# Gate tiles of a mixed attention and recurrence block: all sixteen placed between the steps of the two mixers

## The chip, the core and the metric

The kernel runs on one core of a Trainium2 chip. It uses the five engines of the core: PE (TensorE, matmuls), DVE (VectorE), ACT (ScalarE), POOL (GpSimd) and SP (SyncE, which here only issues DMAs). Each engine works through its own instructions in the order in which they are written and waits on semaphores. The metric is the device time of one execution in microseconds; lower is better.

## The reference, cut to what matters

Two transformer blocks are computed for 512 tokens of width 1024. The part that the change touches is the input projection of the second block's mixer, and the two mixers that use it:

```python
proj = u @ w_in                 # 1024 -> 5256 columns
(q_a, c_kv, q_idx, k_idx, w_idx, q_h, f_h, i_h, g_h, gate_a, gate_b) = split_cols(proj)
# sparse attention: a score per key picks the 128 best keys of each query
dots = einsum('bqhd,bsd->bqhs', qi, k_idx)
score = einsum('bqh,bqhs->bqs', wi, relu(dots)); score = where(causal, score, -inf)
_, idx = lax.top_k(score, 128)
# softmax over the chosen keys, 8 heads, latent values
# recurrence (hgrn2): 4 heads, chunkwise, decay from a running sum of log f
merged = sigmoid(gate_a + b) * (y_a @ w_br_a) + sigmoid(gate_b + b) * (y_b @ w_br_b)
h = h + rms_norm(merged @ w_out, g)
```

The two gates (2048 of the columns) are used only in the last but one line. Nothing in either mixer needs them.

## The kernel before

Activations lie transposed, features on partitions and the 512 tokens along the free axis. A projection is cut into output tiles of 128 columns. A tile takes 8 pieces, one for each 128 inputs, and a piece is three matmuls of 128x512 (high weights by high activations, high by low, low by high, lines 721 to 723 or, in `fill`, 743 to 745), since each operand is split into two parts. The weights of a tile (a unit) are loaded by SP into one of four slots, ACT makes the high part (`w_hi`, L1142) as soon as the tile three before it is finished, and POOL or DVE makes the low part (`w_lo`, L633 on POOL, L1711 and L2278 on DVE).

The second block's input projection has 43 tiles, `TILES2`: numbers 0 to 26 feed the mixers, 27 to 42 are the sixteen gate tiles. The first `LEAD2` tiles are computed one after the other; this is called the front here. Behind a tile, the list `AFTER2` places small work: transposes, latent queries and the index scores. An index score is a matmul of PE (L996), a relu of ACT (L1451) and a multiply-add of DVE (L2161) that adds it to the score. There are 24 of them in 12 pairs: eight for each of the query blocks 3, 2 and 1. Between them DVE picks the best keys of the block just finished: `top8` (L2143 finds eight maxima, L2144 takes them out) 16 times for each block. Before, all 16 rounds for block 1 stand behind the whole front, and `selected(1)` (L2148) ends them.

In the front DVE also moves each mixer tile out of its bank (L2128). ACT works in order too: behind a tile it makes `w_hi`, then waits for DVE's move, applies silu or sigmoid, issues the store, and only then the relus of that tile's index scores.

The sparse attention (35 steps `a`, 8 heads by 4 query blocks) has, in each step on PE, the logits of step a (L1005), the transposes of step a-2 (L1012), the pieces `FILL2[a]` of gate tiles, and the values of step a-3 (L1026); every eighth step a projection (L1036). The logits go to DVE (L2197 adds bias and mask, which POOL prepares at L686), ACT (exponential, L1466), and DVE (L2214, attn). Step 35 of the table has 14 pieces: they stand between the sparse attention and the recurrence.

The recurrence has 36 steps, 4 heads by 9 levels l. On PE each step has the pair matmuls (L1078) and then its pieces; the first step of a head has other pair matmuls ahead (L1065); at level 2 the output of the head before follows the pieces (`hgrn_out`, L1055). POOL makes differences (L663, L665), ACT decays (L1517, L1521, L1522), DVE the factors (L2259, L2260) and keeps the pairs (`keep_pairs`, L2268). At level 4 ACT keeps the output of the head before (L1501), and behind level 5 it takes the logarithm for the next head (`log_forget`, L1507, between two table loads); with it DVE makes the running sums (L2246, three scans) behind level 6.

A finished gate tile costs ACT `keep_gate`: `w_hi` of a later unit, a copy out of the bank (L1410) and the issue of a store. In the recurrence ACT does it two steps after the tile was finished, behind the decay of that step; in the sparse attention one step after.

Of the kernel before, what the change touches and what calls it, by code (L numbers as in the profile page):

```python
# [51 lines left out]
TOPK = 128  # L52
# [17 lines left out]
for _name, _n in (("norm_mix_g", 8), ("norm_ffn_g", 8), ("norm_final_g", 8), ("pool_scale", 4),  # L70
# [10 lines left out]
TILES2 = (["ckv", "kidx", "widx"] + [f"qi{t}" for t in range(4)] + [f"qa{t}" for t in range(4)]  # L81
          + [f"i{t}" for t in range(4)] + [f"qh{t}" for t in range(4)] + [f"gh{t}" for t in range(4)]
          + [f"fh{t}" for t in range(4)] + [f"gate{t}" for t in range(16)])
# [1 line left out]

TILES1 = [(kind, h) for h in range(HEADS) for kind in "qkv"] + [("p", g) for g in range(len(WINDOWS))]
LEAD1 = 3
LEAD2 = TILES2.index("gate0") + 4
STAGES = (("proj1", 16, DC), ("wo", DC, DC), ("up1", 2 * FC, DC), ("down1", 2 * DC, DOWN_CHUNKS),
          ("up2", 2 * FC, DC), ("down2", 2 * DC, DOWN_CHUNKS), ("proj2", len(TILES2), DC),  # L90
          ("branch", 2 * DC, 4), ("out", DC, DC),
# [16 lines left out]
def spread(first_tile, end_tile, rates):  # L108

    steps, at, end = [], first_tile * DC, end_tile * DC  # L110
    for rate in rates:
        pieces, left = [], min(rate, end - at)
        while left:
            n = min(left, DC - at % DC)
            pieces.append((at // DC, at % DC, at % DC + n))
            at, left = at + n, left - n
        steps.append(pieces)
    assert at == end, (at, end)
    return steps


def closed(pieces):
# [6 lines left out]
DSA_STEPS = DSA_HEADS * QB  # L129
HGRN_STEPS = HEADS * len(LEVELS)  # L130
GAP2 = DSA_STEPS + 3
_rates = [1 + (a % 5 == 4) for a in range(GAP2)] + [14]
_left = (len(TILES2) - LEAD2) * DC - sum(_rates)
FILL2 = spread(LEAD2, len(TILES2), _rates + [
    _left * (e + 1) // HGRN_STEPS - _left * e // HGRN_STEPS for e in range(HGRN_STEPS)])
# [78 lines left out]
for _t in range(4):  # L214
    AFTER2[8 + _t] += [("qlat", 2 * _t), ("qlat", 2 * _t + 1)]
    AFTER2[12 + _t].append(("vturn", _t))
_room = TILES2.index("gate0") - 1 - 7
for _s in range(len(IDX_STEPS)):
    AFTER2[7 + _s // 2 * _room // (len(IDX_STEPS) // 2 - 1)].append(("idx", _s))
for _n in AFTER2:  # L220
# [91 lines left out]
def two_blocks(nc, ins, spill, bias_rows, out):  # L312

    with ExitStack() as ctx:
# [162 lines left out]
        def tile_read(stage, i):  # L477
            return tile_sem(stage, i), TILE[stage, i][1] + 1
# [148 lines left out]
        def _(pool):  # L627
# [7 lines left out]
            def split_units(name, start, end):  # L635

                first, size = UNIT[name][0], UNIT[name][2] * P
                loops = max(0, end - start) // SLOTS
                if loops > 1:
                    with pool.Fori(0, loops) as it:  # L640
                        for j in range(SLOTS):
                            split_unit(first + start + j, size, it, SLOTS)
                    start += SLOTS * loops
                for i in range(start, end):
                    split_unit(first + i, size)
# [24 lines left out]
            pool.wait_ge(unit_split, UNIT["proj2"][0] + SLOTS)  # L670
            split_units("proj2", SLOTS, LEAD2 + 3)

# [26 lines left out]
        def _(pe):  # L699
            mm = nc.tensor.matmul  # L700

            def wait(pair):
                pe.wait_ge(pair[0], pair[1])
# [246 lines left out]
            for i in range(AUX_BANKS):  # L950
                wait(tile_read("up2", i))
            for n in range(LEAD2):
                if n == 0:
# [176 lines left out]
        def _(act):  # L1130
# [282 lines left out]

            for n, name in enumerate(TILES2[:LEAD2]):
                kind, t = name.rstrip("0123456789"), int(name[len(name.rstrip("0123456789")):] or 0)
# [222 lines left out]
        def _(dve):  # L1638
# [3 lines left out]
            def step(ins_, it=0, per_loop=0):  # L1642

                steps[0] += 1
                ins_.then_inc(dve_step, 1)
                dve.wait_ge(dve_step, steps[0] + (it * per_loop if per_loop else 0))
# [188 lines left out]
            for name, factor in (("attn_norm_g", 1.0 - LAM_INIT), ("ffn1_post_g", 0.5), ("ffn2_post_g", 0.5)):  # L1835
                first, n = PARAMS[name]
# [294 lines left out]
            def norm_keys(name):  # L2131

                n, src, dst, g = {"ckv": (0, ckv_raw, ckv, "kv_norm_g"),
                                  "kidx": (1, kidx_raw, kidx, "kidx_norm_g")}[name]
                rsqrt(name)
                wait(tile_read("proj2", n))
                v.scalar_tensor_tensor(dst[:, :], src[:, :], prm(g), rstd[:, :], ALU.mult, ALU.mult).then_inc(
                    norm_ready, 1)
                dve.wait_ge(norm_ready, n + 1)

            def top8(i):

                step(v.max(best[:, :], score[i][:, :]))  # L2143
                step(v.match_replace(score[i][:, :], best[:, :], score[i][:, :], TAKEN))  # L2144
# [24 lines left out]
                    if h == DSA_HEADS - 1:  # L2169
                        selected(i + 1)  # L2170
            dve.wait_ge(const2_loaded, 16 * 3)
            for n in range(TILES2.index("gate0")):
                take_tile2(n)
                for ev, m in AFTER2[n]:
                    if ev == "spread":
                        norm_keys(m)
                    elif ev == "wturn":
                        dve.wait_ge(aux_ready, AUX["wturn", 0] + 1)
                        v.tensor_scalar(widx[:, :, :],
                                        aux_bank("wturn", 0)[:, 0:32].rearrange("p (j h) -> p j h", j=QB),  # L2180
                                        IDX_W_SCALE, None, ALU.mult).then_inc(aux_sem("wturn", 0), 1)
                        wait(aux_read("wturn", 0))
                    elif ev == "idx":
                        index_step(m)
            for _r in range(TOPK // 8):
                top8(1)
            selected(1)

            for a in range(DSA_STEPS + 4):
# [156 lines left out]
            for c in range(2):  # L2346
                dve.wait_ge(p_loaded, 32)
                n = SPLIT["p"] + c
# [128 lines left out]
```

## Time and profile before

| | us |
|---|---|
| median of 3 runs | 2026.54 (2024.76 to 2027.18) |
| the profiled execution | 2031.31 |
| its span | 2029.4 |

| engine | busy us | share of the span |
|---|---|---|
| PE | 1861.8 | 92% |
| DVE | 1167.6 | 58% |
| ACT | 648.5 | 32% |
| POOL | 201.2 | 10% |

PE's clock (PEclk) is shown as a share of full speed: 1.0 is 2.4 GHz, 0.5 is 1.2 GHz, and a figure between is a mean over a stretch with both. A wait is idle time of an engine, put down to the instruction that released it. In these profiles the durations of back-to-back matmuls overlap (a matmul of 0.39 us starts every 0.23 us at full clock), so the time of a piece is read from start to start.

### The profile page before, as it was taken

Reading aid. Unit: us, or ns where it says so; the run is one execution under the profiler, and the core shown is the slowest. Engines: PE = TensorE matmul, PEld = TensorE weight load, DVE = VectorE, ACT = ScalarE, POOL = GpSimd, SP = SyncE. Lnnn points to the kernel's source line nnn. Section 1 sums busy time; section 2 is a strip of 40 time slices with the busy share of each in tenths; the row PEclk is TensorE's granted clock in tenths of the full one; section 3 lists DMA queues with packets and bytes.
Section 4 is the critical chain, followed back from the end, with each engine's and each line's share of the span. In section 5 each row is a group of like instructions: output and inputs, shape, how many; then the busy total and the mean of one; then the engine's idle time right before and its main releaser. Section 6 shows DMA issues by size and latency. Waiting matters only on the chain.

```text
span 2029.4 us, 23515 instructions
## 1 busy us (share of the span) xinstructions
PE 1861.8 (92%) x8254; PEld 1489.2 (73%) x8254; DVE 1167.6 (58%) x1772; ACT 648.5 (32%) x960; POOL 201.2 (10%) x150
## 2 busy tenths in 40 slices
PE   5887989999999999999899998877789999999996
PEld 4665777777888888888677776666567788888874
DVE  6447658888534755532443776576683755452266
ACT  4333412222223222222333334444353322222242
POOL 3121000000000000000033344243000000000000
PEclk9888999999999999999899999977899999999997
DMA  3431222223222222323222331310152222232221
GB/s 136 79 67 42 73 80 89 92 92 101 100 98 83 93 93 97 103 100 100 78 83 73 114 129 59 114 68 32 47 161 83 73 96 101 93 119 100 92 71 54
DMA packets 55340, 180.61 MB, mean 89 GB/s; under 512 B 6216, under 2 KB 6984, under 8 KB 55272
## 3 DMA queue, kind: packets, MB, share of 16 engines
q1 hardware_dynamic: 43200, 157.07, 23.2%
q10 hardware_dynamic: 12072, 22.67, 4.0%
q8 instruction: 39, 0.64, 0.1%
q14 instruction: 29, 0.24, 0.0%
HBM read 167.65 MB, written 12.06 MB: 89 GB/s over the span
## 4 chain that ended last, share of the span: by engine, by line
PE 68%; DVE 19%; issue 6%; ACT 3%; DMA 2%; POOL 1%; DVEq 1%; ACTq 0%; SPq 0%; POOLq 0%
PE bank L721 16%; PE bank L722 16%; PE bank L723 16%; PE bank L743 2%; PE bank L744 2%; PE bank L809 2%; PE bank L745 2%; PE bank L810 2%; PE bank L811 2%; DMA raw<-in_w_proj 1%; DVE sq L1990 1%; PE bank L1078 1%; PE bank L789 1%; DVE w_lo L1711 1%; DVE chunk L1809 1%
## 5 line engine op out<-in xcount | busy, mean ns | idle before, releaser
L1142 ACT ACTIVATE w_hi<-raw 128x1024 fp32r<-128x1024 f32 (+2 forms) x281 | 304.4, 1087 | 742.7 <-PE bank L723 677.8
L721 PE MATMUL bank<-a_hi,w_hi 128*128 128x512 f32 x1272 | 504.1, 396 | 17.9 <-DVE w_lo L1711 7.7
L723 PE MATMUL bank<-a_hi,w_lo 128*128 128x512 f32 x1272 | 496.8, 391 | 0.0
L722 PE MATMUL bank<-a_lo,w_hi 128*128 128x512 f32 x1272 | 496.5, 390 | 0.0
L1711 DVE TENSOR_TENSOR w_lo<-raw,w_hi 128x1024 fp32r<-128x1024 f32 (+2 forms) x219 | 280.4, 1281 | 246.7 <-ACT w_hi L1142 234.2
L721 PEld LDWEIGHTS bank<-a_hi,w_hi 128*128 128x128 f32 x1272 | 239.9, 189 | 87.9 <-issue 19.7
L723 PEld LDWEIGHTS bank<-a_hi,w_lo 128*128 128x128 f32 x1272 | 239.7, 188 | 50.7
L722 PEld LDWEIGHTS bank<-a_lo,w_hi 128*128 128x128 f32 x1272 | 240.1, 189 | 49.4 <-issue 1.0
L633 POOL TENSOR_TENSOR w_lo<-raw,w_hi 128x1024 fp32r<-128x1024 f32 x54 | 130.5, 2419 | 1103.9 <-ACT w_hi L1142 1103.9
L721 PE MATMUL bank<-h_hi,w_hi 128*128 128x512 f32 x568 | 221.1, 389 | 0.2 <-DVE w_lo L1711 0.2
L723 PE MATMUL bank<-h_hi,w_lo 128*128 128x512 f32 x568 | 221.0, 389 | 0.0
L722 PE MATMUL bank<-h_lo,w_hi 128*128 128x512 f32 x568 | 221.0, 389 | 0.0
L721 PEld LDWEIGHTS bank<-h_hi,w_hi 128*128 128x128 f32 x568 | 106.6, 188 | 22.8 <-issue 0.6
L723 PEld LDWEIGHTS bank<-h_hi,w_lo 128*128 128x128 f32 x568 | 106.6, 188 | 22.1
L722 PEld LDWEIGHTS bank<-h_lo,w_hi 128*128 128x128 f32 x568 | 106.6, 188 | 21.9
L743 PE MATMUL bank<-a_hi,w_hi 128*128 128x512 f32 x240 | 111.7, 466 | 2.0 <-DVE w_lo L2278 1.2
L744 PE MATMUL bank<-a_lo,w_hi 128*128 128x512 f32 x240 | 99.0, 413 | 0.0
L745 PE MATMUL bank<-a_hi,w_lo 128*128 128x512 f32 x240 | 98.9, 412 | 0.0
L809 PE MATMUL bank<-a_hi,w_hi 128*128 128x512 f32 x144 | 61.6, 428 | 38.8 <-POOL w_lo L633 19.4
L2059 DVE TENSOR_TENSOR val<-bank,rstd 128x512 f32<-128x512 f32 x44 | 30.4, 691 | 115.4 <-PE bank L723 115.4
L1078 PE MATMUL bank<-qk 128*128 128x128 f32 (+1 forms) x256 | 46.2, 330 | 27.6 <-DVE qk L2260 27.5
L809 PEld LDWEIGHTS bank<-a_hi,w_hi 128*128 128x128 f32 x144 | 29.4, 204 | 51.8 <-issue 21.4
(291 smaller groups left out, 2255.3 us busy)
## 6 DMA issues: line engine op xcount, KB each, us to landing
raw<-in_w_up SPq DMA_DIRECT2D x132, 512.0 KB, 3.4
raw<-in_w_down SPq DMA_DIRECT2D x48, 704.0 KB, 4.0
raw<-in_w_proj SPq DMA_DIRECT2D x59, 512.0 KB, 3.5
raw<-in_w_wo SPq DMA_DIRECT2D x8, 512.0 KB, 3.4
raw<-in_w_branch SPq DMA_DIRECT2D x16, 256.0 KB, 2.7
gates_in<-spill ACTq DMA_DIRECT2D x16, 256.0 KB, 3.0
raw<-in_w_out SPq DMA_DIRECT2D x8, 512.0 KB, 4.3
raw<-in_w_ple SPq DMA_DIRECT2D x8, 512.0 KB, 3.5
```

What stands on the lines that cost most here:

```text
L633: pool.tensor_tensor(lo, src, hi.bitcast(F32), ALU.subtract).then_inc(unit_split, 1)
L721: mm(dst[:, :], wh, hi[:, k, :], start=(first and c == 0), stop=False)
L722: mm(dst[:, :], wh, lo[:, k, :], start=False, stop=False)
L723: step = mm(dst[:, :], wl, hi[:, k, :], start=False, stop=(last and c == n - 1))
L743: mm(dst[:, :], wh, a_hi[:, c, :], start=(c == 0), stop=False)
L744: mm(dst[:, :], wh, a_lo[:, c, :], start=False, stop=False)
L745: step = mm(dst[:, :], wl, a_hi[:, c, :], start=False, stop=(c == DC - 1))
L809: mm(dst[:, :], wh, hi[:, k, :], start=(k == 0), stop=False)
L810: mm(dst[:, :], wh, lo[:, k, :], start=False, stop=False)
L1078: step = mm(dst[:, col:col + n], qk[:, e % 2, j * P:(j + 1) * P], qk[:, e % 2, q0:q0 + n], start=True, stop=True)
L1142: fn(w_hi[:, slot, 0:size], raw[:, slot, 0:size], ACT.Copy).then_inc(unit_high, 1)
L1711: v.tensor_tensor(w_lo[:, slot, 0:size], raw[:, slot, 0:size], w_hi[:, slot, 0:size].bitcast(F32), ALU.subtract).then_inc(unit_split, 1)
```

## The change

`LEAD2` becomes 27 instead of 31: the front ends with the last mixer tile, and all sixteen gate tiles are computed piece by piece between the steps. The table of pieces changes with it. The sparse attention gets 1 piece in even steps and 2 in odd ones, 52 in all (before 42: 2 in each fifth step, else 1). The 14 pieces of step 35 stay. The recurrence gets 62 pieces (before 40), which is 1 or 2 in a step: by level 1 2 2 1 2 2 2 1 2 in heads 0 and 2, and 2 1 2 2 2 1 2 2 2 in heads 1 and 3 (before 1 1 1 1 1 1 1 1 2 in each).

The 12 pairs of index scores stand behind tiles 7 8 10 11 13 14 16 17 19 20 22 24 (before 7 8 10 12 13 15 17 19 20 22 24 26), and the 16 rounds of `top8` for block 1 stand behind tiles 25 and 26, eight behind each. The tiles, their banks and SP's queue are the same.

```diff
-LEAD2 = TILES2.index("gate0") + 4
+LEAD2 = TILES2.index("gate0")
...
-_rates = [1 + (a % 5 == 4) for a in range(GAP2)] + [14]
+_rates = [1 + a % 2 for a in range(GAP2)] + [14]
...
-_room = TILES2.index("gate0") - 1 - 7
+_room = LEAD2 - 3 - 7
...
-            for n in range(TILES2.index("gate0")):
+            for n in range(LEAD2):
                 take_tile2(n)
...
-            for _r in range(TOPK // 8):
-                top8(1)
+                for _r in range(TOPK // 16 if n >= LEAD2 - 2 else 0):
+                    top8(1)
             selected(1)
```

DVE at the end of the front. Before, block 2 is finished and the rounds of block 1 (score_113) follow at once, both evictions being long done:

```order
L2148 TENSOR_SCALAR score_114<-score_114 128x384
L2143 MAX best<-score_113 128x8
L2144 MATCH_REPLACE score_113<-best,score_113 128x256
L2143 MAX best<-score_113 128x8
L2144 MATCH_REPLACE score_113<-best,score_113 128x256
```

Now the eviction of tile 25 stands in between:

```order
L2148 TENSOR_SCALAR score_114<-score_114 128x384
L2128 TENSOR_TENSOR gate<-bank,rstd_mix 128x512
L2143 MAX best<-score_113 128x8
L2144 MATCH_REPLACE score_113<-best,score_113 128x256
```

The eviction of tile 26 stands eight rounds later. The index scores ahead of this place have moved two tiles forward.

PE in head 1 of the recurrence, levels 1 and 2 (qk are the factors of a level, bank1 holds the gate tile). Before, one piece of three matmuls stands behind each pair matmul, and hgrn_out (pair_d by v2) follows:

```order
L1078 MATMUL bank5<-qk_135 128x128 x4
L743 MATMUL bank1<-a_hi_53,w_hi_51 128x512
L744 MATMUL bank1<-a_lo_54,w_hi_51 128x512
L745 MATMUL bank1<-a_hi_53,w_lo_50 128x512
L1078 MATMUL bank6<-qk_135 128x128 x4
L743 MATMUL bank1<-a_hi_53,w_hi_51 128x512
L744 MATMUL bank1<-a_lo_54,w_hi_51 128x512
L745 MATMUL bank1<-a_hi_53,w_lo_50 128x512
L1055 MATMUL bank2<-pair_d_136,v2_101 128x128 x2
L1055 MATMUL bank2<-pair_1_137,v2_101 128x128
```

Now level 2 has two pieces ahead of hgrn_out, as level 0 has:

```order
L1078 MATMUL bank5<-qk_135 128x128 x4
L743 MATMUL bank1<-a_hi_53,w_hi_51 128x512
L744 MATMUL bank1<-a_lo_54,w_hi_51 128x512
L745 MATMUL bank1<-a_hi_53,w_lo_50 128x512
L1078 MATMUL bank6<-qk_135 128x128 x4
L743 MATMUL bank1<-a_hi_53,w_hi_51 128x512
L744 MATMUL bank1<-a_lo_54,w_hi_51 128x512
L745 MATMUL bank1<-a_hi_53,w_lo_50 128x512
L743 MATMUL bank1<-a_hi_53,w_hi_51 128x512
L744 MATMUL bank1<-a_lo_54,w_hi_51 128x512
L745 MATMUL bank1<-a_hi_53,w_lo_50 128x512
L1055 MATMUL bank2<-pair_d_136,v2_101 128x128 x2
```

What moved: six more pieces stand in this head, at levels 0, 2, 3, 4, 6 and 7.

ACT in head 1, levels 4 to 6. Before, the kept output (oh, sq) and the decay of level 5 are followed by the logarithm (silu<-hf, between its table loads) and the decays of level 6:

```order
L1501 ACTIVATE oh<-bank 128x512
L1186 ACTIVATE sq<-oh 128x512
L1517 ACTIVATE decay<-diff 128x512
L1507 ACT_TABLE_LOAD
L1507 ACTIVATE silu<-hf 128x512
L1521 ACT_TABLE_LOAD
L1521 ACTIVATE decay<-diff 128x4x64
```

Now the work for a finished gate tile stands in between:

```order
L1501 ACTIVATE oh<-bank 128x512
L1186 ACTIVATE sq<-oh 128x512
L1517 ACTIVATE decay<-diff 128x512
L1142 ACTIVATE w_hi<-raw 128x1024
L1410 ACTIVATE gate<-bank 128x512
L1412 DMA spill<-gate 128x512
L1507 ACT_TABLE_LOAD
L1507 ACTIVATE silu<-hf 128x512
L1521 ACT_TABLE_LOAD
L1521 ACTIVATE decay<-diff 128x4x64
```

It stands at the same place in head 0. In head 2, where such work stood there before, it now stands behind the decays of level 6.

## Rows read from the trace of the kernel before

**Rows 1.** The page, part 4: the chain that ended last, shares by engine.

```profile
PE 68%; DVE 19%; issue 6%; ACT 3%; DMA 2%; POOL 1%; DVEq 1%; ACTq 0%; SPq 0%; POOLq 0%
```

**Rows 2.** Busy time by stretch of the span; columns as its header row says.

```profile
core 0: us, PE busy (x) PEld busy (x) DVE busy (x) ACT busy (x) POOL busy (x), PEclk, DMA share, GB/s
1106.00:1190.00 84.00, 79.82 (x357) 61.69 (x355) 60.79 (x113) 28.52 (x42) 31.15 (x13) 0.99 0.36 119
1190.00:1218.80 28.80, 26.81 (x108) 21.55 (x108) 23.94 (x67) 10.33 (x14) 12.45 (x7) 0.91 0.36 128
1218.80:1303.50 84.70, 72.54 (x398) 55.09 (x399) 60.11 (x163) 42.34 (x110) 36.70 (x35) 0.98 0.18 57
1323.00:1446.00 123.00, 93.99 (x504) 80.78 (x504) 82.60 (x128) 49.62 (x86) 42.74 (x60) 0.82 0.12 41
1422.60:1443.80 21.20, 20.47 (x142) 18.32 (x142) 13.92 (x25) 8.84 (x18) 4.72 (x7) 1.00 0.13 37
```

**Rows 3.** Waits of DVE, 1106 to 1218.5 us: total us, times, longest us.

```profile
DVE score L2161 <- ACT relu L1451: 19.1, 6, 3.7
DVE score L2158 <- ACT relu L1451: 2.8, 2, 1.5
```

**Rows 4.** Timeline, DVE, ACT and PE, end of the front: start us, us, what, [idle before].

```profile
1189.88 0.69 DVE L2128 TENSOR_TENSOR gate<-bank,rstd_mix 128x512 f32<-128x512 f32 x1
...
1190.60 0.63 ACT L1427 ACTIVATE gate<-gate 128x512 f32<-128x512 f32 x1 [6.45 <-DVE gate L2128]
...
1190.62 0.79 PE L721 MATMUL bank<-a_hi,w_hi 128*128 128x512 f32 x1 [4.80 <-DVE gate L2128]
...
1192.07 0.63 PE L721 MATMUL bank<-a_hi,w_hi 128*128 128x512 f32 x1
...
1193.35 0.63 PE L721 MATMUL bank<-a_hi,w_hi 128*128 128x512 f32 x1
...
1194.14 1.33 DVE L2161 SCALAR_TENSOR_TENSOR score<-relu,widx,score 128x256 f32<-128x256 f32 x1 [2.97 <-ACT relu L1451]
...
1197.57 0.39 PE L721 MATMUL bank<-a_hi,w_hi 128*128 128x512 f32 x1
...
1198.25 0.39 PE L721 MATMUL bank<-a_hi,w_hi 128*128 128x512 f32 x1
...
1217.99 0.45 DVE L2148 TENSOR_SCALAR score<-score 128x256 f32<-128x256 f32 x1
...
1221.83 0.30 PE L1012 MATMUL bank<-ident,attn 128*128 128x128 f32 x1 [4.39 <-DVE attn L2214]
```

**Rows 5.** Waits in the sparse attention, 1218.8 to 1303.5 us: PE's, then DVE's.

```profile
PE bank L1012 <- DVE attn L2214: 13.5, 10, 4.4
...
DVE logit L2197 <- PE bank L1005: 12.4, 11, 1.8
DVE logit L2197 <- PE bank L1012: 6.3, 7, 1.5
```

**Rows 6.** Waits in the recurrence, 1323 to 1446 us: PE's, DVE's, ACT's.

```profile
PE bank L1078 <- DVE qk L2260: 27.5, 15, 5.8
...
DVE pair_d L2268 <- PE bank L1065: 15.5, 3, 5.7
...
ACT oh L1501 <- PE bank L1055: 11.0, 3, 5.0
```

**Rows 7.** Timeline, recurrence, ACT, PE and DVE: start us, us, what, [idle before].

```profile
1374.12 1.04 ACT L1142 ACTIVATE w_hi<-raw 128x1024 fp32r<-128x1024 f32 x1
...
1375.06 1.21 PE L1078 MATMUL bank<-qk 128*128 128x128 f32 x8 [2.14 <-DVE qk L2260]
...
1399.98 0.61 ACT L1142 ACTIVATE w_hi<-raw 128x512 fp32r<-128x512 f32 x1
...
1405.51 0.88 DVE L2259 TENSOR_TENSOR qk<-hk,decay 128x256 f32<-128x256 f32 x1 [3.49 <-issue]
...
1406.87 2.05 PE L1078 MATMUL bank<-qk 128*128 128x128 f32 x8 [3.52 <-DVE qk L2260]
```

## The prediction

> **What bounds the kernel now.** I read the chain of waits first, by engine: PE holds 68% of it and DVE 19% [rows 1]. So PE's work, and what PE waits for, set the end. Then I read the stretches that the change touches [rows 2]. In the front, 1106 to 1190, PE is busy 79.82 of 84.00 us. From 1190 to 1218.8 it is busy 26.81 of 28.80, but with work that nobody waits for, the four gate tiles, while DVE finishes the choice of keys (23.94 busy). The sparse attention (1218.8 to 1303.5) has PE busy 72.54 of 84.70 us, at a clock of 0.98, and the recurrence (1323 to 1446) 93.99 of 123.00 at a mean clock of 0.82. PE's idle time lies there, 12 and 29 us, and the question is how much of the four tiles fits into it.
>
> The reader should see two prices in the timeline at the end of the front [rows 4]. A piece, from the start of L721 to the next, takes 0.68 us at full clock (1197.57 to 1198.25), and 1.28 us at half clock (1192.07 to 1193.35), where PE starts again after a wait of 4.80 us. And the front does not end with PE: DVE's last instruction for the choice (L2148) is at 1217.99, and PE waits 4.39 us until 1221.83 for the first attn.
>
> **The front.** Four tiles leave it, 32 pieces, 21.8 us of PE at full clock. None of this is saved as such, since the sparse attention starts when DVE is done. What counts is how much sooner DVE is done. Its work is the same: the same evictions, 24 multiply-adds and 48 rounds. Only its idle time can shrink. From 1106 to 1218.8 that is 28 us (112.8 less 60.79 and 23.94 busy) [rows 2], of which 21.9 us are waits for relus, 19.1 and 2.8 [rows 3]; the rest is waits for PE and short gaps. The cause is visible [rows 4]: DVE evicts fh2 at 1189.88 and fh3 behind it, ACT only then starts (0.63 us at 1190.60), stores, does the next, and the relu comes so late that DVE resumes at 1194.14 after 2.97 idle us. This order on ACT is unchanged. I went through the new order by hand. Of the pairs from tile 13 on, the one at tile 14 follows a tile without silu and finds its relus ready; those at 17 and 20 stand behind a single eviction, where the relu is some 1.8 us late instead of 3.0 to 3.7 (estimate: one silu, one issue and half a pair of relus less); 16, 19, 22 and 24 wait 3.5 to 4.3. Their sum is about 20 us, 2 less than before, and about 2 us of waits for PE's tiles go as well, since DVE is then behind PE. I take **-4 us**. The ends are 0 (the waits only move) and -22 (all waits for relus go). The eight rounds behind tile 25 do not stall anything: by then PE's tile 26 is finished or in work, and its bank is another.
>
> PE's restart at the head of the sparse attention stays. Now it comes after 4.39 us of idle time, later after some 25 us. A wait of 4.80 us is enough to bring PE back at half clock, as the pieces at 1192.07 and 1193.35 show [rows 4], so I count nothing more for the longer one; 2 us is the upper end (three pieces at 1.28 instead of 0.68).
>
> Here a rule speaks against the change. The Trainium skill, "TensorE: Matmul & The Clock Gate", section "HAM oscillation — how this bites in real kernels", says that an array with long idle gaps falls back to half rate and pays a restart after each. By the rule alone the new gap would be charged those 2 us; by the rows the old gap had already paid them. The trace agrees with the rule as far as the restart at 1190.62 goes [rows 4].
>
> **The sparse attention.** Ten pieces more, 6.8 us of PE. PE waits 13.5 us in 10 places there, 4.4 of it at the start [rows 5], so about 9 us could take them; but DVE waits for PE's logits as well, 12.4 and 6.3 us, so PE and DVE hold each other. It depends on the step. The waits of PE come mostly at steps with a%4 = 0. A second piece in a%4 = 3 stands just ahead of one and is mostly hidden: 7 more pieces, of which I count 1.3 us. In a%4 = 1 it delays the logits of the next block, which DVE waits for: 7 more pieces, 4.8 us. Four even steps lose a piece, -2.5. The sum is **+3.5 us**; ends 0 and 6.8. POOL has two more splits here and ACT one or two more tiles to keep. POOL is busy 36.70 of 84.70 us, ACT 42.34, so I cost them at nothing; if a split of POOL got in front of a mask that DVE wants, it would cost up to 2.4 us each.
>
> **Between.** The 14 pieces, the loads of the recurrence and its first scans are unchanged: nothing.
>
> **The recurrence.** 22 pieces more, 15 us at full clock, and three more tiles for ACT to keep. PE waits here 27.5 us in 15 places for the factors [rows 6], which looks like room for everything. But the waits lie in the wrong levels. DVE waits 15.5 us, 3 times, for the pair matmuls that open a head (L1065), and ACT 11.0 us, 3 times, for hgrn_out (L1055). So in each head PE's pieces at levels 7 and 8 and at levels 0 to 2 are on the path, and those at 3 to 6 are beside it: there the path goes through ACT, from the kept output over decay, two table loads and the logarithm to the level 6 decays, and then through DVE's scans. By head:
> - Head 0 has no hgrn_out; its added pieces at 1, 2, 4, 5 and 6 meet small waits, and the first piece need no longer wait for its low part: +0.5.
> - Head 1: levels 0 (partly at half clock, 1.0), 2 (0.7) and 7 (half, 1.3): +3.0.
> - Head 2: levels 1 and 2: +1.4.
> - Head 3: there is no next head to prepare, and PE is busy 20.47 of 21.20 us at full clock [rows 2]; six pieces are 4.1 us, less 0.7 of idle time: +3.4.
>
> That makes 8.3 us. Then ACT. Keeping a tile costs w_hi 1.04 us [rows 7], a copy of some 0.6 and the issue with its gap, 2.1 us in all. In heads 0 and 1 this now stands just ahead of the logarithm. The trace has this case in head 2: ACT does w_hi at 1399.98 (a small unit, 0.61 us) between decay and logarithm, DVE's factors come 3.49 us late at 1405.51, and PE waits 3.52 us at 1406.87, where in head 1, without such work, it waits 2.14 (1375.06) [rows 7]. So twice +2.1, and -1.5 in head 2, where the work moves behind the level 6 decays and under the scans: +2.7. Two more splits on DVE (1.2 us each) fall where it waits anyway. The recurrence gives **+11 us**; its ends are -5 (a higher clock, below) and +18 (every piece at full price and the 2.7).
>
> **The sum.** -4 + 3.5 + 11 = +10.5 us. The profiled execution was 2031.31 us, with 1.9 outside its span; it would become 2041.8. It is 4.8 us above the median of the runs, 2026.54, and I expect the same difference of the runs: **2037.0 us**. What a measurement can tell from no change is 0.2%, 4.1 us.
>
> **Rivals.**
> - *DVE stops waiting in the front (faster).* If closer pairs let each relu be ready when DVE gets to it, all 22 us of waits go, DVE is done near 1196, and the change is -22 + 3.5 + 11 = -7.5: 2019.0 us. For it: DVE is busy 60.79 of 84.00 us only [rows 2], and the pairs stand closer. Against it: ACT's relu stands behind DVE's eviction of the same tile, whatever the distance. It decides from a gain of 14.5 us in the front upwards (3.5 + 11): below that the mixers take it back.
> - *The clock stays up in the recurrence (no change).* The mean clock of 0.82 over 123.00 us means about 44 us at half rate. If the denser pieces shorten the waits ahead of level 6 (2.14 and 3.52 us [rows 7]) so that the clock no longer falls after them, and half of those 44 us run at full rate, PE is 11 us sooner. The sum is -4 + 3.5 + 11 - 11 = -0.5: 2026.0. For it: in head 3, without long waits, the clock is 1.00. Against it: the scans keep their wait, and ACT's added work lengthens those of heads 0 and 1.
> - *Nothing is hidden (slower still).* 6.8 in the attention, 15 and 2.7 in the recurrence, and a second of POOL's splits in the way, 2: +22.5 with the front's -4, 2049 us. For it: PE and DVE wait for each other in both mixers. Against it: 27.5 us of waits, some of which must take in the added pieces.
> - *The front gains 10, the recurrence loses 7:* +0.5, 2027. Each term is at its good side, but no mechanism of its own stands behind it.
>
> **How the numbers follow.** My own forecast 0.60, with a range of 2030 to 2043; the faster front 0.10; the clock 0.12; nothing hidden 0.10; the mixed case 0.08. Ends that hold 8 in 10: 2024 to 2047. Faster by over 0.2%: the first rival and a third of the clock's, 0.14. Within 0.2%: 0.08 of the clock's and 0.07 of the mixed case, 0.15. Slower: mine, nothing hidden and 0.01 of the mixed case, 0.71.
>
> **What would show it.** In the changed kernel: DVE's L2148 for block 1 at about 1213 to 1215, with waits for relus of 18 to 20 us; PE idle from about 1187 until then; the sparse attention 3 to 4 us longer than 84.7, with PE's waits for attn down to 8 or so; the recurrence 10 us or more longer than 123, with PE's waits in it smaller, DVE's waits for L1065 longer, and the level 6 factors of heads 0 and 1 later by 2 us. If the mean clock there rises above 0.9, the second rival is right. If L2148 comes before 1206, the first is. A front that ends later than now would prove my pass over it wrong.

## The result and the profile after

The changed kernel takes 2036.83 us (median of 5 runs, 2035.63 to 2038.77), the kernel before 2026.54 (5 runs): ratio 1.0057, 95% interval 1.0043 to 1.0071, so 10.3 us slower. Forecast were 2037.0. The sum hides a loss that I had at nothing, a gain that I had too small and a loss that I had too large.

To see where the time went I cut the span at the same instructions in both traces. The profiled executions took 2038.77 us (after) and 2031.31 (before), 1.9 and 4.8 above their medians: they are 7.5 us apart where the medians are 10.3, so the table holds some 3 us less than there is to explain.

| stretch, from the first instruction of one line to that of the next | before | after | difference | forecast |
|---|---|---|---|---|
| ahead of the front | 1041.4 | 1039.6 | -1.8 | 0 |
| front: first scaling of the latent keys on DVE to the first logit, L2197 | 177.4 | 170.4 | -7.0 | -4 |
| sparse attention: to the last value projection, L1036 | 91.0 | 95.6 | +4.6 | +3.5 |
| gap: to the first L1065 | 10.0 | 20.3 | +10.3 | 0 |
| first scans and factors: to the first L1078 | 7.0 | 4.0 | -3.0 | 0 |
| recurrence: to the last hgrn_out, L1055 | 116.8 | 119.3 | +2.5 | +11 |
| behind it, to the end of the span | 585.8 | 587.6 | +1.8 | 0 |

The stretches of the changed kernel, with the columns of the header row:

```profile
core 0: us, PE busy (x) PEld busy (x) DVE busy (x) ACT busy (x) POOL busy (x), PEclk, DMA share, GB/s
1106.00:1210.00 104.00, 85.78 (x365) 65.75 (x363) 83.66 (x179) 31.73 (x47) 33.98 (x15) 0.92 0.29 101
1210.00:1218.80 8.80, 5.67 (x18) 3.89 (x18) 6.17 (x18) 2.79 (x9) 4.10 (x5) 0.60 0.00 0
1210.00:1305.70 95.70, 84.51 (x461) 64.97 (x461) 63.09 (x163) 46.28 (x116) 41.77 (x37) 0.96 0.20 67
1305.70:1329.90 24.20, 13.56 (x54) 10.46 (x51) 7.83 (x12) 7.43 (x9) 4.77 (x8) 0.78 0.55 206
1329.90:1425.20 95.30, 73.60 (x410) 62.58 (x410) 67.52 (x101) 40.27 (x68) 32.69 (x45) 0.91 0.16 54
1425.20:1449.40 24.20, 24.16 (x160) 21.91 (x160) 14.65 (x26) 8.80 (x18) 4.89 (x7) 1.00 0.12 41
```

The fourth row is the surprise: 24.20 us with PE busy 13.56. The last row is head 3, with PE full, as before in 21.20 us [rows 2].

**Front.** DVE's waits in the changed kernel, 1106 to 1210 (total us, times, longest), and the timeline at its end (start us, us, what, idle before):

```profile
DVE score L2161 <- ACT relu L1451: 11.9, 5, 3.0
DVE score L2158 <- ACT relu L1451: 4.2, 2, 3.0
```

```profile
1192.71 0.69 DVE L2128 TENSOR_TENSOR gate<-bank,rstd_mix 128x512 f32<-128x512 f32 x1
...
1209.64 0.29 DVE L2148 TENSOR_SCALAR score<-score 128x256 f32<-128x256 f32 x1
1209.96 0.29 DVE L2197 TENSOR_TENSOR logit<-bank,sum_sq 128x128 f32<-128x128 f32 x1
...
1213.13 0.44 PE L1012 MATMUL bank<-ident,attn 128*128 128x128 f32 x1 [16.24 <-DVE attn L2214]
...
1213.23 0.77 PE L743 MATMUL bank<-a_hi,w_hi 128*128 128x512 f32 x1
1213.80 0.63 PE L744 MATMUL bank<-a_lo,w_hi 128*128 128x512 f32 x1
```

The waits for relus are 16.1 us against 21.9 [rows 3], 5.8 less where I had 2, and L2148 stands at 1209.64 where I had 1213 to 1215 (before: 1217.99 [rows 4]). PE waits 16.24 us, not some 25, since it has work until 1196.9 where I had 1187, and starts at half clock (0.63 us a matmul; mean 0.60 in the second row above). The Trainium skill, "TensorE: Matmul & The Clock Gate", section "HAM oscillation — how this bites in real kernels", says that a long gap is paid for with a restart; this trace agrees (0.63 us a matmul behind 16.24 us without work), and e4_rec72 below has the price.

**Between.** The end of the gap in the changed kernel, ACT, PE and DVE:

```profile
1313.14 0.91 DVE L2228 MEMSET pair_d<- 128x1024 f32 x1 [5.40 <-DMA resets<-in_c_resets]
...
1315.57 3.45 DVE L2246 TENSOR_TENSOR_SCAN run<-resets,silu 128x512 f32<-128x512 f32 x3 [0.30 <-ACT silu L1507]
...
1321.99 1.04 ACT L1142 ACTIVATE w_hi<-raw 128x1024 fp32r<-128x1024 f32 x1
1322.94 0.58 ACT L1410 ACTIVATE gate<-bank 128x512 f32<-128x512 f32 x1
...
1323.57 0.80 PE L743 MATMUL bank<-a_hi,w_hi 128*128 128x512 f32 x1 [8.94 <-ACT gate L1410]
...
1326.30 1.91 PE L1065 MATMUL bank<-hq,hk 128*128 128x128 f32 x8
1328.24 0.72 DVE L2268 COPY_PREDICATED pair_d<-masks,bank 128x512 f32<-128x512 int32 x1 [9.22 <-PE bank L1065]
```

Read it from below. DVE waits 9.22 us for the first pair matmuls, these stand behind two pieces, and the first of these waits 8.94 us until ACT has copied a gate tile out of its bank. The gate tiles share two banks in turn. Before, 42 + 14 = 56 pieces are seven whole tiles, and the 14 of step 35 finish the seventh. Now 52 + 14 = 66: the 14 finish tiles 33 and 34 and put two pieces into tile 35, whose bank is that of tile 33. ACT empties tile 33 only in the recurrence, behind the decay of its step 1, and that decay needs DVE's scans. The 14 pieces were unchanged; where they stand against the tile's end was not.

**Recurrence.** Starts of level 0 (L1078), head by head, one execution each:

| | head 0 | head 1 | head 2 | head 3 | PEclk, heads 0 to 2 |
|---|---|---|---|---|---|
| before, 40 pieces | 32.2 | 30.4 | 33.2 | 21.3 | 0.78 |
| after, 62 | 32.8 | 32.6 | 29.9 | 24.2 | 0.91 |

Head 3 is longer by 2.9 (forecast 3.4). Heads 0 to 2 have 16 pieces more and are together half a microsecond shorter (forecast 7.6 longer).

### The profile page after: what moved, and what is told of

It reads as the page before. It is cut to its first block, busy times and chain, and to the rows that moved or that the text cites. A ratio compares the mean times of both kernels' runs of the same rounds, so it can differ in the third digit from the quotient of the medians.

```text
span 2036.8 us, 23512 instructions
## 1 busy us (share of the span) xinstructions
PE 1855.9 (91%) x8254; PEld 1484.8 (73%) x8254; DVE 1171.5 (58%) x1774; ACT 648.6 (32%) x960; POOL 196.3 (10%) x148
## 4 chain that ended last, share of the span: by engine, by line
PE 68%; DVE 20%; issue 6%; DMA 3%; ACT 3%; DVEq 1%; POOL 1%; ACTq 0%; SPq 0%; POOLq 0%
PE bank L721 16%; PE bank L723 16%; PE bank L722 16%; PE bank L743 2%; PE bank L745 2%; PE bank L744 2%; PE bank L809 2%; PE bank L810 2%; PE bank L811 2%; DMA raw<-in_w_proj 2%; DVE score L2144 1%; DVE best L2143 1%; DVE sq L1990 1%; PE bank L1078 1%; PE bank L789 1%
## 5 line engine op out<-in xcount | busy, mean ns | idle before, releaser
L721 PEld LDWEIGHTS bank<-a_hi,w_hi 128*128 128x128 f32 x1240 | 234.2, 189 | 81.0 <-issue 20.4
L723 PEld LDWEIGHTS bank<-a_hi,w_lo 128*128 128x128 f32 x1240 | 234.3, 189 | 50.0
L722 PEld LDWEIGHTS bank<-a_lo,w_hi 128*128 128x128 f32 x1240 | 234.4, 189 | 48.3 <-issue 1.0
L633 POOL TENSOR_TENSOR w_lo<-raw,w_hi 128x1024 fp32r<-128x1024 f32 x52 | 125.8, 2420 | 1102.4 <-ACT w_hi L1142 1102.4
L723 PEld LDWEIGHTS bank<-h_hi,w_lo 128*128 128x128 f32 x568 | 106.6, 188 | 21.9
L2059 DVE TENSOR_TENSOR val<-bank,rstd 128x512 f32<-128x512 f32 x44 | 30.4, 690 | 115.6 <-PE bank L723 115.6
L743 PEld LDWEIGHTS bank<-a_hi,w_hi 128*128 128x128 f32 x272 | 54.1, 199 | 24.8 <-ACT gate L1410 9.4
L809 PEld LDWEIGHTS bank<-a_hi,w_hi 128*128 128x128 f32 x144 | 29.6, 206 | 48.3 <-issue 20.6
```

What stands on the lines that cost most here:

```text
L633: pool.tensor_tensor(lo, src, hi.bitcast(F32), ALU.subtract).then_inc(unit_split, 1)
L721: mm(dst[:, :], wh, hi[:, k, :], start=(first and c == 0), stop=False)
L722: mm(dst[:, :], wh, lo[:, k, :], start=False, stop=False)
L723: step = mm(dst[:, :], wl, hi[:, k, :], start=False, stop=(last and c == n - 1))
L743: mm(dst[:, :], wh, a_hi[:, c, :], start=(c == 0), stop=False)
L809: mm(dst[:, :], wh, hi[:, k, :], start=(k == 0), stop=False)
```

## The experiments

Three theories went in: A, the bank wait makes the loss of the gap; B, the pieces in the mixers lie on the path as forecast; C, the loss comes from PE standing idle at the end of the front, where it had four gate tiles to do before. Each result has the kernel before as run on the same chip beside it: 2027.07 (e1 to e4), 2026.62 (e5 to e8), 2026.03 (e9, e10, e12), 2025.38 (e13).

### e1_gap12 and e2_keep33: the bank

```diff
-_rates = [1 + a % 2 for a in range(GAP2)] + [14]
+_rates = [1 + a % 2 for a in range(GAP2)] + [12]
```

> The changed kernel with 12 instead of 14 pieces between the mixers; the recurrence gets 64 instead of 62. Theory A (bank): the last 2 of the 14 pieces open tile 35, which needs the bank of tile 33, and ACT empties that bank only in the recurrence. The 12 pieces end with tile 34, so the wait of 8.94 us goes and the first pair matmuls no longer stand behind it. The recurrence starts 9 to 10 us sooner: 2026 to 2029 us. Theory B (pieces in the recurrence are on its path, as predicted): two more pieces there cost 1 to 2 us: 2038 us. Theory C (the loss is the front's missing cover, the idle PE): no change, 2037 us.

```diff
+            early = closed(FILL2[GAP2])[:1]
+            for t in early:
+                keep_gate(t)
             log_forget(0)
...
-                            keep_gate(t)
+                            if t not in early:
+                                keep_gate(t)
```

> The changed kernel with its 14 pieces, but ACT copies tile 33 out of its bank before the first logarithm of the recurrence, not two steps into it. PE's order is the same. Theory A (bank): PE's wait of 8.94 us goes to under 1 us: 2026 to 2029 us. Theories B and C: no change, 2035 to 2039 us; ACT's two us fall into its wait for the loads.

Measured: e1 2027.41 us, ratio to before 1.0000 [0.9991, 1.0008]; e2 2030.79, 1.0019 [1.0010, 1.0028]. The first pair matmuls and the first factors of e1, with PE released by DVE's keys and DVE waiting for nothing from PE:

```profile
1316.94 1.13 PE L1065 MATMUL bank<-hq,hk 128*128 128x128 f32 x8 [0.74 <-DVE hk L2239]
1317.10 3.46 DVE L2246 TENSOR_TENSOR_SCAN run<-resets,silu 128x512 f32<-128x512 f32 x3 [0.30 <-ACT silu L1507]
1320.47 0.70 DVE L2268 COPY_PREDICATED pair_d<-masks,bank 128x512 f32<-128x512 int32 x1
```

Gap and first factors are 16.9 us in e1 and 16.7 in e2, as before (17.0), against 24.3 in the changed kernel. e2 changes nothing but when the bank is emptied: the wait costs 6.0 us by the medians. e1 came within theory A's range of 2026 to 2029, e2 1.8 us above it and 4.2 below the range of B and C. So A has the cause, and its size was too large: the loss of the gap is 7.3 us in the traces and 6.0 by the medians, not 9 to 10. The rest of e1's gain is the next experiment's term.

### e5_defer: ACT's tile ahead of the logarithm

e2_keep33, and the tiles due at level 5 are kept behind the decays of level 6 (the diff is against e2_keep33):

```diff
-                        for t in closed(FILL2[GAP2 + e - 1]):
+                        late = closed(FILL2[GAP2 + e - 2]) if l == 6 else []
+                        for t in late + (closed(FILL2[GAP2 + e - 1]) if l != 5 else []):
```

> The changed kernel with tile 33 kept by ACT before the first logarithm (as in e2_keep33, 2030.79 us), and with ACT's keep_gate of level 5 moved behind the decays of level 6. In heads 0 and 1 it no longer stands between decay and logarithm. Theory ACT (my prediction: such a tile costs 2.1 us of the path, twice): 4.2 us less than e2_keep33, 2026.6. Theory beside (PE's own work sets those heads, so that factors that come 2 us sooner are taken up 2 us later by PE): within 1 us of e2_keep33, 2030 to 2031.5. Trace: by theory ACT, PE's longest wait for factors in heads 0 and 1 shrinks from some 3.5 to some 1.5 us.

Measured: 2027.60 us, 3.2 below e2 (expected by theory ACT 4.2 below, by its rival at most 1). Head 1, first e2, then e5: level 6's factors and pair matmuls.

```profile
1365.85 1.06 ACT L1142 ACTIVATE w_hi<-raw 128x1024 fp32r<-128x1024 f32 x1 [0.50 <-PE bank L745]
...
1371.83 0.88 DVE L2263 TENSOR_TENSOR qk<-hk,decay 128x256 f32<-128x256 f32 x1 [4.51 <-ACT decay L1525]
...
1373.20 1.13 PE L1078 MATMUL bank<-qk 128*128 128x128 f32 x4 [3.51 <-DVE qk L2264]
```

```profile
1367.15 1.04 ACT L1142 ACTIVATE w_hi<-raw 128x1024 fp32r<-128x1024 f32 x1
...
1367.33 0.88 DVE L2264 TENSOR_TENSOR qk<-hk,decay 128x256 f32<-128x256 f32 x1 [2.10 <-ACT decay L1525]
...
1368.69 1.13 PE L1078 MATMUL bank<-qk 128*128 128x128 f32 x8 [1.09 <-DVE qk L2265]
```

PE's wait falls from 3.51 to 1.09. Heads 0 and 1 are 2.5 and 2.4 us shorter, head 2 1.4 longer though nothing was moved in it, 3.5 in all, close to the medians (3.2). e1 needs neither mend, since its tiles end elsewhere, and agrees with e5: 2027.4 and 2027.6. So after (2036.8) is e1 plus the bank (6.0) plus this term (3.2).

### e3_old_front: what the front gained, and from what

The changed table, but index scores and the 16 rounds placed as before.

```diff
-_room = LEAD2 - 3 - 7
+_room = LEAD2 - 1 - 7
...
-                for _r in range(TOPK // 16 if n >= LEAD2 - 2 else 0):
-                    top8(1)
+            for _r in range(TOPK // 8):
+                top8(1)
```

> The changed kernel with index scores and rounds of block 1 as before (pairs up to tile 26, all 16 rounds behind the front); sixteen gate tiles still between the steps. The traces give the new front 7 us (the first logits 8.9 us sooner, of which 1.8 were there before the front). If that is the placement: 2043 to 2044 us. If it came from the absence of the four gate tiles (fewer evictions in the way, fewer low parts on POOL): 2037 us.

Measured: 2044.37 us, 7.5 above the changed kernel. DVE's waits in its front:

```profile
DVE score L2161 <- ACT relu L1451: 19.2, 6, 3.7
DVE score L2158 <- ACT relu L1451: 2.8, 2, 1.5
```

These are those of before, 22.0 and 21.9, though the four gate tiles are gone. The front is 176.5 us, 0.9 under before. So 6.1 of the 7.0 us came from the new places of index scores and rounds, and taking the tiles out of the front gave 0.9. e3 moves scores and rounds back together and does not part the two; of the gain, 5.9 us are waits for relus (22.0 less 16.1), which speaks for the scores. e6 below agrees from the other side: it has the new places and two gate tiles in the front, and its front takes 170.8 us.

### e4_rec72: attention as before, 72 pieces in the recurrence

```diff
-_rates = [1 + a % 2 for a in range(GAP2)] + [14]
+_rates = [1 + (a % 5 == 4) for a in range(GAP2)] + [14]
```

> The changed kernel with the old table in the sparse attention (42 pieces) and 14 between; the recurrence gets 72 pieces, two in every step. The 14 pieces end with tile 33, so no bank is waited for. Theory A, with pieces in the recurrence hidden (the trace after gives it 0 us for 22 of them) and 10 in the attention costing 4.7: 2026.5 - 7 + 1 = 2019 to 2022 us. Theory B (pieces on the path in the recurrence, 0.5 us each): 32 pieces cost 14 to 16 us and the attention nothing: 2033 to 2036 us.

Measured: 2030.22 us, ratio 1.0015 [1.0006, 1.0024]. It lies between the two ranges, 2019 to 2022 and 2033 to 2036, so neither theory holds as it was put. Its attention is 91.9 us: 3.7 less than with ten more pieces (95.6), and 0.9 more than before. PE waits 16.95 us ahead of it, but the length of that wait is not what the 0.9 is for: e6 and e9 below have the same pieces in the attention behind waits of 4.62 and 4.61 us, and it takes 91.7 us there. The long wait makes 0.2 of it; what the other 0.7 are is open. Its recurrence is 123.2 us. With the front at -7, the 32 more pieces cost the recurrence 6.4 us in the trace and about 9 by the medians, 0.2 to 0.3 a piece, where a piece is 0.68 [rows 4]; in that is one tile kept ahead of a logarithm.

### e7_beside and e8_on_path: do the levels matter?

e1_gap12, the same 64 pieces in the recurrence, placed by level:

```diff
-    _left * (e + 1) // HGRN_STEPS - _left * e // HGRN_STEPS for e in range(HGRN_STEPS)])
+    (1, 1, 1, 3, 3, 3, 2, 1, 1)[e % 9] for e in range(HGRN_STEPS)])
```

> e1_gap12 (2027.41 us) with its 64 pieces of the recurrence placed by level: 3 each at levels 3, 4 and 5, 2 at level 6, 1 at the others, in each head. By my prediction levels 3 to 6 lie beside the path and 0 to 2, 7 and 8 on it: 11 pieces of each head beside it, 5 on it, where the even table has some 7 and 9. Four pieces of 0.68 us less on the path per head: 10.9 us less at most, 2017 to 2023 if most of it comes. By the theory that what counts is how much of PE's work there is, wherever it stands: within 1.5 us of e1_gap12. By the theory that factors and PE's work are bound to each other at levels 3 to 6 (PE late at level 6 delays the bank that DVE waits for): 3 to 6 us more than e1_gap12.

e8_on_path has (3, 2, 3, 1, 1, 1, 1, 2, 2) there.

> e1_gap12 (2027.41 us) with its 64 pieces at 3, 2, 3 on levels 0 to 2, 2 and 2 on levels 7 and 8, 1 on each of 3 to 6: 12 pieces of each head on the path by my prediction, 4 beside it, where the even table has 9 and 7. My prediction: three pieces more on the path per head, 0.68 us each, 8 us more in all: 2033 to 2036. By the theory that the amount of work alone counts: within 1.5 us of e1_gap12. Together with e7_beside, which has 7 pieces of each head on the other side: the two differ by 19 us if the levels were as I said, by less than 2 if they do not matter.

Measured: 2019.69 us (ratio 0.9972 [0.9961, 0.9983]) and 2039.22 (1.0066 [1.0053, 1.0080]). The same work, with 28 of the 64 pieces in other places, is worth 19.5 us, 0.70 us a piece; expected were 19. e7 came within its 2017 to 2023; e8 missed its 2033 to 2036 by 3.2. PE in heads 0 to 2, e7 and then e8:

```profile
1322.20:1408.70 86.50, 72.30 (x416) 62.24 (x417) 69.86 (x101) 42.42 (x72) 33.61 (x48) 0.94 0.20 65
```

```profile
1322.90:1427.00 104.10, 78.53 (x416) 67.05 (x417) 68.29 (x101) 42.78 (x72) 32.55 (x48) 0.87 0.17 56
```

PE is idle 14.2 us in the one and 25.6 in the other; the remaining 6 are a lower clock. Head 3 does not care: 24.6 and 24.9, since PE is full there at every level. So my map of the levels is right for heads 0 to 2, and one price for each piece is not. The 21 pieces that differ there are worth 17.6 us in the traces, and against e1 (91.5 us in heads 0 to 2, PE busy 73.0, clock 0.94) e7 saves 5.0 us with 12 pieces off the path, while e8 loses 12.6 with nine more on it: 0.4 and 1.4 us a piece. Of the 12.6, 7.1 are idle time of PE and 5.5 are matmuls at the lower clock. That the mean over all 28 comes out at the 0.68 of a piece is in part luck.

### e12_copies: what is the clock worth?

The kernel before, with the pieces of levels 3 to 5 issued three times over: 24 copies, which spoil the gate sums.

```diff
...
-                    fill("proj2", FILL2[GAP2 + 1 + e])
+                    fill("proj2", FILL2[GAP2 + 1 + e], 3 if 3 <= e % 9 <= 5 else 1)
```

> The kernel before, with its own 40 pieces in the recurrence where they are, but the matmuls of each piece at levels 3, 4 and 5 of each head issued three times over: 24 copies, 16 us of PE at full clock, that do nothing useful (the gate sums count these pieces three times). It asks what the clock is worth. All changed kernels are 3.3 to 7.4 us shorter in the recurrence than 0.64 us for each piece on the path says, and their mean clock there is 0.89 to 0.95 as against 0.82. Clock theory: more work beside the path lifts the clock, and with it every matmul on the path: 3 to 5 us LESS than before with more work, 2022 to 2024, clock in the recurrence 0.90 or more. Theory of cover alone: the copies lie in waits, 0 to +2 us, 2027 to 2029, and the clock changes nothing. If levels 3 to 5 are on the path after all: +10 us or more.

Measured: 2029.08 us, ratio 1.0019 [1.0008, 1.0029], 3 us MORE than before. Its executions spread from 2026.13 to 2035.17, and the profiled one took 2034.85. Heads 0 to 2 before, then heads 0 to 2 and head 3 of e12 (head 3 before: 21.2 [rows 2]):

```profile
1326.80:1422.60 95.80, 73.46 (x363) 62.44 (x363) 66.29 (x100) 38.25 (x66) 34.53 (x48) 0.78 0.11 36
```

```profile
1326.60:1422.40 95.80, 78.86 (x416) 67.05 (x416) 66.93 (x100) 38.41 (x65) 34.39 (x48) 0.86 0.10 36
1422.40:1446.60 24.20, 24.13 (x160) 21.91 (x160) 14.02 (x25) 8.93 (x18) 4.72 (x7) 1.00 0.11 33
```

18 copies, 12 us of PE at full clock, cost nothing in heads 0 to 2, and the 6 in head 3 cost 2.9. PE is busy only 5.4 us more in heads 0 to 2, so the matmuls of before took some 7 us less there at the higher clock (estimate: 73.46 and 12.2 less 78.86), and the heads are as long as before. The clock rose and made the kernel no faster: theory clock, as I had written it for this run, fell in its time. Its condition was not met in full: the clock over the four heads is 0.89, where I had asked for 0.90 or more and the changed kernel has 0.93, so e12 is a weaker lift than the change itself. Cover alone explains the time, at the upper end of its 2027 to 2029. A lift by the clock that the copies use up again is not excluded.

### e6_lead29, e9_lead29_lv, e10_ext, e13_both: towards a better version

e6: two gate tiles stay in the front, index scores close together as in the changed kernel, attention table of before, gap 14, recurrence 56. The diff is against the changed kernel.

```diff
-LEAD2 = TILES2.index("gate0")
+LEAD2 = TILES2.index("gate0") + 2
...
-_rates = [1 + a % 2 for a in range(GAP2)] + [14]
+_rates = [1 + (a % 5 == 4) for a in range(GAP2)] + [14]
...
-_room = LEAD2 - 3 - 7
+_room = TILES2.index("gate0") - 3 - 7
...
-            for n in range(LEAD2):
+            for n in range(TILES2.index("gate0")):
                 take_tile2(n)
...
-                for _r in range(TOPK // 16 if n >= LEAD2 - 2 else 0):
+                for _r in range(TOPK // 16 if n >= TILES2.index("gate0") - 2 else 0):
                     top8(1)
```

> Two gate tiles stay in the front (of four before), index scores and top-k as close together as in the changed kernel, the 42 pieces in the sparse attention placed as before, 14 pieces in the gap (they now end with a tile), 56 in the recurrence as against 42 before and 64 in e1_gap12. If the terms measured so far add up: front -7, attention 0, gap 0, recurrence +1 to +3, against the kernel before at 2027.1: 2021 to 2023 us. If the gain of the front needs an empty PE (the two tiles put the choice of keys back by their own 11 us): front 0, so 2028 to 2030. If it is the sum of pieces in the two mixers alone that counts, at the 0.2 us a piece that e4_rec72 showed (32 pieces, 6.4 us): 14 pieces are 2.8 us, and with the front 2022.9.

Measured: 2023.31 us, 0.9987 [0.9978, 0.9996]. Front 170.8, attention 91.7, gap 10.0, recurrence 117.1: the terms add up, and the two tiles do not disturb the front. The third sum, 0.2 us for each piece in the mixers (2022.9), fits as well; this run does not part it from the first. PE waits 4.62 us ahead of the attention here, and its clock falls all the same:

```profile
1215.17 0.30 PE L1012 MATMUL bank<-ident,attn 128*128 128x128 f32 x1 [4.62 <-DVE attn L2214]
1215.22 0.62 PE L743 MATMUL bank<-a_hi,w_hi 128*128 128x512 f32 x1
1215.64 0.63 PE L744 MATMUL bank<-a_lo,w_hi 128*128 128x512 f32 x1
```

e9 is e6 with (1, 0, 1, 3, 3, 3, 2, 1, 0) in the recurrence, e10 is e1 with (0, 0, 0, 4, 4, 4, 3, 1, 0).

> e6_lead29 (2023.3 us; two gate tiles in the front) with its 56 pieces of the recurrence placed per head as 1, 0, 1 on levels 0 to 2, 3, 3, 3, 2 on levels 3 to 6, 1, 0 on levels 7 and 8: 12 pieces of the recurrence on the path where the even table has 32. At the 0.64 us for a piece on the path that e8_on_path and e7_beside give (28 pieces, 17.9 us in the recurrence) 20 pieces less are 12.8 us less, 2010.5; at the 7.7 us that e7_beside gained over e1_gap12 with 16 pieces less on the path, 9.6 us less, 2013.7. I take 2012. If levels 3 to 6 are full at the three pieces of e7_beside and levels 0 to 2, 7 and 8 have nothing left to give below one piece: 2018 to 2020, no better than e7_beside.

> e7_beside (2019.7 us) pushed further: 64 pieces per head as 0, 0, 0, 4, 4, 4, 3, 1, 0, so 4 pieces in all on levels 0 to 2, 7 and 8 as against 20. At 0.64 us a piece 10 us less, 2009.5. If three pieces already fill the waits at levels 3 to 5 (a fourth delays the next level's pair matmul and with it the bank that DVE's factors wait for), the price of the fourth takes it back: 16 pieces beside which cost as much as on the path, 2019 to 2021. Trace: by the first, PE's waits for factors (20.3 us in e7_beside) shrink to about 12 at unchanged length of DVE's own work; by the second they stay and move to levels 0 to 2.

Measured: e9 2024.23 us, 12 from what I took and outside the range of its rival too; e10 2021.64, 0.6 above the range of its second theory. e10's trace shows where the empty levels go, PE at levels 2 and 3 of head 0 and level 1 of head 1:

```profile
1329.68 1.13 PE L1078 MATMUL bank<-qk 128*128 128x128 f32 x8 [1.88 <-DVE qk L2260]
1331.80 2.04 PE L1078 MATMUL bank<-qk 128*128 128x128 f32 x8 [0.99 <-DVE qk L2260]
...
1355.10 1.31 PE L1078 MATMUL bank<-qk 128*128 128x128 f32 x5 [0.76 <-DVE qk L2260]
```

A level without a piece waits for its factors 0.8 to 1.9 us, no less than the 0.68 of a piece, so the first piece of such a level is covered and only the second is paid for. Heads 0 to 2 of e10 are as long as those of e7 (86.3 and 86.5 us) with 12 pieces off the path; its loss is in head 3, 1.9 us longer. e9 has such waits too (1.29 us at level 1 of head 2), and in head 2 one of its tiles ends so that ACT keeps it ahead of the logarithm, the case of e5:

```profile
1388.78 1.06 ACT L1142 ACTIVATE w_hi<-raw 128x1024 fp32r<-128x1024 f32 x1 [0.48 <-PE bank L745]
1389.74 0.58 ACT L1410 ACTIVATE gate<-bank 128x512 f32<-128x512 f32 x1
...
1390.71 1.28 ACT L1507 ACT_TABLE_LOAD   x1 [0.39 <-ACT gate L1410]
```

That does not make up 12 us; how the rest divides stays open. With 16 pieces a head, as in e7, each tile ends at the same two levels of every head. e13 keeps that: e7's table and 64 pieces, two tiles in the front, 42 pieces in the attention, and what is left, 6, in the gap.

> e7_beside (2019.69 us) with two gate tiles left in the front, as in e6_lead29, so that the sparse attention has its 42 pieces as before, the gap 6 pieces in place of 12, and the recurrence the same 64 at the same levels. What the runs so far say: attention 52 to 42 pieces, 95.6 to 91.7 us, 3.9 less; front 0 (170.4 and 170.8); gap 0, since DVE's chain (resets, keys, scans, 5.2 us of wait for the resets alone) sets the first factors, and PE's pieces there only cover it; recurrence 0 (the same table, and tiles that close at the same levels). Sum 2016 us, with a restart of PE at half clock after an idle stretch of some 5 us 2017. If the recurrence reacts to where its tiles close and to the clock as e9_lead29_lv did (2024.2 where 2012 was expected): 2020 or more.

Measured: **2015.45 us** (2014.85 to 2017.00), ratio 0.9953 [0.9939, 0.9966], 10 us under before and 21 under the changed kernel. Front 170.5, attention 91.9, gap 9.5 with half the pieces of e7, recurrence 111.5: each as expected.

## Why the prediction was right or wrong

The time came out, by luck: errors of +6.0 (the gap), -4.3 (the pieces in the recurrence), -3.5 (the front) and +1.6 (attention and ACT) met. By medians the terms of the 10.3 us are: front -7.5 (after less e3), bank +6.0 (after less e2), ACT's tiles ahead of the logarithm +3.2 (e2 less e5), and a remainder of 8.6, of which 4.6 is the attention in the traces and so some 4 the pieces in the recurrence. The runs were taken on different chips. With each set against the kernel before on its own chip, the first three are -7.0, +6.6 and +2.7, and some 3 are left for the pieces. So each is good to 1 or 2 us.

- **"Between ... unchanged: nothing."** Wrong, and the step that failed: +6.0. I counted the 14 pieces and not the tiles that they belong to. The order shows it: a piece that opens a tile waits for the bank of the tile before the last, and the instruction that frees it stood in the recurrence. PE waited 8.94 us there. My rivals had no such case either.
- **Front, -4.** Right in sign and cause, too small: -7.0 in the trace, -7.5 by medians. My "2 less" for the relus measured 5.8; the waits are at most 3.0 us each where I had 3.5 to 4.3. The first rival (all 22 us go) did not come.
- **PE's restart.** "I count nothing more": right. The attention with the pieces of before takes 91.9 us behind a wait of 16.95 us (e4) and 91.7 behind 4.62 (e6). It takes 91.0 before, behind 4.39; those 0.7 us are not the length of the wait, and stay open. The idle time itself was 16.24 us, not 25.
- **Sparse attention, +3.5.** 3.7 for the ten pieces, 4.6 with the 0.9 of e4. PE's waits for attn behind the first, 23.4 less 16.2, are 7.2; I had 8 or so:

```profile
PE bank L1012 <- DVE attn L2214: 23.4, 8, 16.2
```

- **ACT's keep_gate, +2.7.** The 2.7 are twice 2.1 for heads 0 and 1, less 1.5 for head 2. e5 moves only the first two: 4.2 forecast, 3.2 measured, and the heads themselves gave 2.5 and 2.4. The place is the one that I named (PE waits 3.51 at level 6 in head 1). Right in mechanism; the -1.5 of head 2 was not tested.
- **Pieces in the recurrence, +8.3.** Mis-sized: about 4 by medians. Head 3 is right (2.9 to 3.4). In heads 0 to 2 I had 4.9 and about 1 came by the medians, and in the traces they got shorter. The levels are on and beside the path as I said (e7, e8), but the price of a piece on the path is not one number: it was 0.4 us from e1 to e7 and 1.4 from e1 to e8. I charged the second piece of levels 1, 2 and 7 its full time, part of it at half clock (1.3 at level 7 of head 1), where the clock was then up. That this is what made the term too large is argued and not shown. One sign also failed: DVE's waits for L1065 in the recurrence, which I had longer, are 11.8 us against 15.5.
- **The second rival, the clock.** "If the mean clock there rises above 0.9, the second rival is right": it rose from 0.82 to 0.93 (0.78 to 0.91 in heads 0 to 2, 1.00 in head 3 both times), and PE's work in heads 0 to 2 is as long as before (73.60 and 73.46 us busy) with 16 pieces more. So its condition was met, and even its 11 us are there as busy time of PE: 16 pieces are 10.9 us at full clock. They did not come off the length, which shrank by half a microsecond with those pieces taken in, and e12 lifted the clock in the kernel before and gained nothing. How much of the 4.3 us by which the term of the pieces was too large is the clock, and how much is cover by waits, stays open; the profiled execution of before is itself 4.8 us above its median. The sum fits because this, the front and the loss in the gap happen to cancel.

## What to carry to other kernels

When work is dealt out in pieces between steps, compare not only how many pieces stand in a place but which buffer each opens and which instruction frees it: a piece that opens a buffer carries a wait with it. Ask of each step whether the engine has slack there before dealing evenly; 28 pieces moved between steps were worth twice what the whole change cost. And let a forecast that hits by its sum be checked by its stretches: here errors of +6, -4.3 and -3.5 all but cancelled.

## What was not expected of the hardware

A rise of the granted clock is not a gain in itself. In e12 the mean in heads 0 to 2 went from 0.78 to 0.86 with PE busy 78.86 us in place of 73.46, over the same 95.8 us. And the length of an idle stretch hardly showed in the restart: after 16.24 us PE's matmuls took 0.63 us up to 1216.64 and 0.40 at 1217.12, some 4 us at half clock, and before, after 4.80 us [rows 4], they took 0.63 from 1191.21 to 1194.20 and 0.40 at 1195.05, some 4 us as well. In the attention the two lengths, 16.95 us (e4) and 4.62 (e6), differ by 0.2 us.
